# Feed-forward stages of a two-block transformer: modulation rows gathered in one open PSUM bank and turned once per stage

## What is computed

```python
def swiglu(x, w_gate, w_up, w_down):
    return (jax.nn.silu(x @ w_gate) * (x @ w_up)) @ w_down
x = x + 0.5 * swiglu(rms_norm(x, g[0]), ffn_w_gate[layer, 0], ...)
```

```python
sh1, sc1, g1, sh2, sc2, g2 = split_mod(silu(c) @ w_mod[i] + b_mod[i], (B, 1))
ch1, cc1, cg1, ch2, cc2, cg2 = split_mod(silu(c_ctx) @ w_mod[i] + b_mod[i], (1, 1))
```

## Time and profile before

| | |
|---|---|
| median of 3 runs | 4479.57 us |
| lowest and highest run | 4478.26 and 4483.99 us |
| time of the profiled execution | 4477.89 us |
| its span, first to last instruction | 4475.9 us |
| mean granted TensorE clock over the span | 0.962 |
| PE busy | 4127.0 us (92%) |
| PEld busy | 3776.9 us (84%) |
| DVE busy | 3072.6 us (69%) |
| ACT busy | 1807.9 us (40%) |
| moved from and to HBM | 783.44 MB, mean 175 GB/s |

### The profile page before, as it was taken

The page is one execution under the profiler, slowest core; times in us unless marked ns, Lnnn a source line. Parts: engine busy times, 40 slices in busy tenths (PEclk is TensorE's granted clock), DMA queues, the critical chain, the costliest instruction groups (busy, mean ns, idle before and its releaser), DMA issues. The chain is left out here.

```text
span 4475.9 us, 80834 instructions
## 1 busy us (share of the span) xinstructions
PE 4127.0 (92%) x30028; PEld 3776.9 (84%) x30028; DVE 3072.6 (69%) x5251; ACT 1807.9 (40%) x2650; POOL 37.9 (1%) x54
## 2 busy tenths in 40 slices
PE   8978999969988589999999899999997889999998
PEld 8956999949974389899888798998886589899887
DVE  5575565545532637988788588878884659887887
ACT  4324343334331434444333444443333444444333
POOL 0000000000000001000000010000000001000000
PEclk9988999989999989999999999999998999999999
DMA  6633766517530037655777476557772157556775
GB/s 230 211 121 107 229 201 226 184 46 228 170 115 19 4 122 206 194 176 177 227 234 235 157 219 188 177 176 233 235 235 83 43 172 229 170 174 197 235 235 184
DMA packets 299941, 783.44 MB, mean 175 GB/s; under 512 B 32800, under 2 KB 133152, under 8 KB 298912
## 3 DMA queue, kind: packets, MB, share of 16 engines
q1 hardware_dynamic: 299680, 779.81, 56.5%
HBM read 728.29 MB, written 51.38 MB: 174 GB/s over the span
## 5 line engine op out<-in xcount | busy, mean ns | idle before, releaser
L248 ACT ACTIVATE ring_hi<-ring 128x1024 fp32r<-128x1024 f32 x1163 | 1232.7, 1061 | 1926.4 <-PE banks L269 1236.1
L254 DVE TENSOR_TENSOR ring_lo<-ring,ring_hi 128x1024 fp32r<-128x1024 f32 x1163 | 1423.6, 1225 | 658.7 <-ACT ring_hi L248 643.3
L265 PE MATMUL banks<-h_parts,ring_hi 128*128 128x256 f32 x4824 | 1222.5, 291 | 106.2 <-ACT ring_hi L248 104.9
L266 PE MATMUL banks<-h_parts,ring_hi 128*128 128x256 f32 x4824 | 1199.5, 286 | 0.0
L265 PEld LDWEIGHTS banks<-h_parts,ring_hi 128*128 128x128 f32 x4824 | 937.6, 194 | 120.5 <-issue 70.7
L266 PEld LDWEIGHTS banks<-h_parts,ring_hi 128*128 128x128 f32 x4824 | 939.0, 195 | 0.3
L280 PE MATMUL banks<-h_parts,ring_hi 128*128 128x512 f32 x3048 | 763.6, 392 | 0.3 <-DVE h_parts L1681 0.3
L269 PE MATMUL banks<-h_parts,ring_lo 128*128 128x256 f32 x4824 | 681.9, 284 | 0.9 <-DVE ring_lo L254 0.6
L280 PEld LDWEIGHTS banks<-h_parts,ring_hi 128*128 128x128 f32 x3048 | 548.2, 189 | 99.4 <-issue 1.4
L269 PEld LDWEIGHTS banks<-h_parts,ring_lo 128*128 128x128 f32 x4824 | 627.3, 193 | 2.5 <-DVE ring_lo L254 2.5
L283 PEld LDWEIGHTS banks<-h_parts,ring_lo 128*128 128x128 f32 x3048 | 415.8, 190 | 29.7
(11 more groups left out here) (213 smaller groups left out, 3746.6 us busy)
## 6 DMA issues: line engine op xcount, KB each, us to landing
ring<-peer_u_dram SPq DMA_DIRECT2D x384, 512.0 KB, 4.1
ring<-peer_v_dram SPq DMA_DIRECT2D x384, 512.0 KB, 4.2
act_store<-acts_out SPq DMA_DIRECT2D x384, 128.0 KB, 3.2
scratch<-act_store SPq DMA_DIRECT2D x384, 128.0 KB, 3.8
ring<-ffn_gate_dram SPq DMA_DIRECT2D x88, 512.0 KB, 3.9
ring<-ffn_up_dram SPq DMA_DIRECT2D x88, 512.0 KB, 3.7
ring<-ffn_down_dram SPq DMA_DIRECT2D x88, 512.0 KB, 3.7
big<-mod_w_dram SPq DMA_DIRECT2D x80, 512.0 KB, 4.6
```

The source lines that it names most:

```text
L248: self.nc.scalar.activation(self.hi[:, n % 2], self.ring[:, self.slot(j)], ACT.Copy).then_inc(self.count("tile_hi").sem, 1)
L254: self.nc.vector.tensor_tensor(self.lo[:, self.slot(j)], self.ring[:, self.slot(j)], self.hi[:, n % 2].bitcast(F32), ALU.subtract).then_in ...
L265: self.nc.tensor.matmul(out, w, b_hi, start=opens and m == 0, stop=False)
L266: self.nc.tensor.matmul(out, w, b_lo, start=False, stop=False)
```

## The change

`modulate(g)` keeps its eight matmuls, but their weights are a window of 32 columns that begins 8 - 2g columns ahead of chunk c's block of 32, in which the two columns of c now stand at 8 and 9. So c and c_ctx appear in columns 2g and 2g + 1 of the window, and each group adds into two rows of its own, the other rows receive zeros. No matmul has `start` set any more: bank 6 is opened with the other four at the start of the stage, and all five groups add into it. It no longer waits for the copy of the group before.

Copy, turn and bias happen once for a stage, at `kept_at = L + 1` = 21: one copy of bank 6, four turning matmuls whose moving operand `side` has 10 columns in place of 2, and on DVE five bias adds, one for each group, each reading two of every ten columns of bank 7. `vec` and `con` grow by 8 columns each: `after_lam`, zeros behind `lam` into which the last windows reach, and the wider `side`.

```diff
-    ("c", KD * 2), ("ev_sink", 8), ("swa_sink", 16), ("lam", 4 * HD),
+    ("c", KD * 2), ("ev_sink", 8), ("swa_sink", 16), ("lam", 4 * HD), ("after_lam", 8),
...
-for _name, _n in (("ident", P), ("block", P), ("rot", P), ("iota", P), ("cos", T), ("sin", T), ("side", 2)):
+for _name, _n in (("ident", P), ("block", P), ("rot", P), ("iota", P), ("cos", T), ("sin", T), ("side", 10)):
...
-        return self.v("lam").rearrange("p (c m) -> p c m", m=32)
+        return self.v("lam").rearrange("p (c m) -> p c m", m=32)[:, :, 8:10]
+
+    def c_in_row(self, c, g):
+        first = VEC["lam"][0] + 32 * c + 8 - 2 * g
+        return self.vec[:, first:first + 32]
...
-    def group_kept(f):
-        return group_made(f - 1) if f else None
+    kept_at = L + 1
...
             def modulate(g):
-                pe.wait_ge(copied.sem, copied.after(g))
                 pe.wait_ge(landed[g % 2].sem, landed[g % 2].after(16 * RING * (g // 2 + 1)))
                 for c in range(KD):
                     q, r, m = c % 4, c // 2, c % 2
-                    last = nc.tensor.matmul(k.ps[32 * q:32 * q + 32, 6], c_wide[:, c],
-                                            mod_w[g % 2][:, r, m * RING * P:(m + 1) * RING * P], start=c < 4, stop=c >= 4)
+                    last = nc.tensor.matmul(k.ps[32 * q:32 * q + 32, 6], k.c_in_row(c, g),
+                                            mod_w[g % 2][:, r, m * RING * P:(m + 1) * RING * P], start=False,
+                                            stop=g == G - 1 and c >= 4)
                 last.then_inc(modded.sem, 1)
-            def turn(g):
-                pe.wait_ge(copied.sem, copied.after(g + 1))
-                pe.wait_ge(taken.sem, taken.after(g))
+            def turn():
+                pe.wait_ge(copied.sem, copied.after(1))
                 for r in range(RING):
-                    last = nc.tensor.matmul(k.ps[:, 7, 2 * r:2 * r + 2], k.scratch[:, r * P:(r + 1) * P],
+                    last = nc.tensor.matmul(k.ps[:, 7, 2 * G * r:2 * G * (r + 1)], k.scratch[:, r * P:(r + 1) * P],
                                             k.c("side"), start=True, stop=True)
                 last.then_inc(turned.sem, 1)
-            k.open_banks(range(4))
+            k.open_banks((0, 1, 2, 3, 6))
             for f in range(FT):
                 rise(f)
                 if f:
                     fall(f - 1)
-                if group_kept(f) is not None:
-                    turn(group_kept(f))
+                if f == kept_at:
+                    turn()
                 if group_made(f) is not None:
                     modulate(group_made(f))
...
-                g = group_kept(f)
-                if g is not None:
-                    act.wait_ge(modded.sem, modded.after(g + 1))
-                    act.wait_ge(turned.sem, turned.after(g))
+                if f == kept_at:
+                    act.wait_ge(modded.sem, modded.after(G))
                     nc.scalar.activation(k.scratch[:, 0:RING * P], k.ps[:, 6], ACT.Copy).then_inc(copied.sem, 1)
...
-                g = group_kept(f)
-                if g is not None:
-                    at = groups[g] * RING
-                    dve.wait_ge(turned.sem, turned.after(g + 1))
-                    nc.vector.tensor_tensor(mods[:, at:at + RING], k.ps[:, 7, 0:2 * RING].rearrange("p (r m) -> p r m", m=2),
-                                            bias[:, at:at + RING].unsqueeze(2).to_broadcast([P, RING, 2]),
-                                            ALU.add).then_inc(taken.sem, 1)
+                if f == kept_at:
+                    dve.wait_ge(turned.sem, turned.after(1))
+                    rows = k.ps[:, 7, 0:2 * L].rearrange("p (r g m) -> p r g m", g=G, m=2)
+                    for g in range(G):
+                        at = groups[g] * RING
+                        last = nc.vector.tensor_tensor(mods[:, at:at + RING], rows[:, :, g],
+                                                       bias[:, at:at + RING].unsqueeze(2).to_broadcast([P, RING, 2]), ALU.add)
+                    last.then_inc(taken.sem, 1)
```

More of the change, by code:

```diff
@@ L82, in _constants @@
     put("iota", np.broadcast_to(i, (P, P)))
-    put("side", i[:, None] % 32 == np.arange(2))
+    put("side", i[:, None] % 32 == np.arange(10))
     t = np.arange(T)
@@ L714, in swiglu @@
     acc = k.ps[:, 0:4].rearrange("p b (c t) -> p (b c) t", t=T)
-    c_wide = k.c_wide()
     mods, bias = k.mods[:].rearrange("p l n m -> p (l n) m"), k.v("b_mod")
     mod_w = [k.region(8192 + s * RING * D, RING, D) for s in range(2)]
-    assert L < FT - 1
+    assert L < FT - 1 and len(set(groups)) == 5
     def gate_at(f):
@@ L806, in _ @@
             if gain is not None:
-                pe.wait_ge(taken.sem, taken.after(G))
+                pe.wait_ge(taken.sem, taken.after(1))
                 for c in range(KD):
@@ L887, in swiglu @@
         s.ends(FT)
-    for s in (modded, copied, turned, taken):
-        s.ends(G)
+    modded.ends(G)
+    for s in (copied, turned, taken):
+        s.ends(1)
     for m in range(2):
@@ L1808, in _ @@
             dve.wait_ge(copied.sem, copied.after(2))
-            nc.vector.tensor_copy(k.c_wide()[:, :, 0:2], k.v("c").rearrange("p (c m) -> p c m", m=2))
+            nc.vector.tensor_copy(k.c_wide(), k.v("c").rearrange("p (c m) -> p c m", m=2))
         @block.scalar
@@ L2044, in layouts @@
         "c": np.stack([_columns(i["c_2"]), _columns(i["c_ctx_2"])], axis=-1).reshape(P, -1),
-        "ev_sink": rows(_paired(i["ev_sinks"], 8, 4)), "swa_sink": rows(_paired(i["swa_sink_2"], 16, 4)), "lam": rows(i["diff_lambda_2"]),
+        "ev_sink": rows(_paired(i["ev_sinks"], 8, 4)), "swa_sink": rows(_paired(i["swa_sink_2"], 16, 4)), "lam": rows(i["diff_lambda_2"]), "after_lam": np.zeros((P, 8), np.float32),
     }
```

## The result

The changed kernel took 4450.89 us (median of 6 runs, 4443.15 to 4456.26) against 4478.91 us (median of 6, 4476.13 to 4483.99) for the one before: ratio 0.9935, 95% interval 0.9922 to 0.9948. The direction was right, the size was not.

A forecast was written before the change was run, and what follows sets the result against it. PE's instruction queue was taken to bound the four feed-forward stages; -14.5 for turns, +0.9 for opening matmuls and +1.3 for adds gave -12.3 us, from 4479.6 to about 4467 us, range about 4461 to 4475.

The forecast's parts named there:

- the wider constants: Loads of `vec` and `con` 4 KB longer, under 0.1 us, and tiles behind them shifted by 64 bytes: both taken as 0.
- Removed turns: 16 of 20 turns leave PE's queue in the four feed-forward stages, 0.905 us each: -14.5 us.
- opening: One more opening matmul on PE at each of four stage starts, 0.21 us each: +0.9 us.
- adds: Four more bias adds on DVE ahead of the last low part at each stage's end, 0.08 us each: +1.3 us.
- Copies and adds taken off ACT and DVE at no gain: 16 copies on ACT and 16 bias adds on DVE removed inside the stages: nothing gained, since both engines have slack.
- Columns of the turn: The turn at a stage's end has 10 moving columns in place of 2: at most 0.4 us, taken 0.
- Products unchanged: The 20 groups keep 16 passes each on PE, 2.05 us a group: change taken as 0.
- third rival: Products in a group run one after the other, not side by side: +97 us, 4564 us in all; chance 0.03.
- first rival: TensorE's clock falls after the longer pause at all four stage ends: 4.3 us more, gain 8.0, 4471.6 us; chance 0.08.
- second rival: PE waits for `ring_hi` where it now turns: time near 4479.6 us, plus up to 2 us; chance 0.08.

The follow-up runs named there:

- the kernel with only this part: The changed kernel with 192 bytes left free ahead of `hidden_parts`, so that it begins on a multiple of 256 bytes again: 4467.49 us, ratio 0.9975.
- the repetition: The changed kernel measured and profiled once more, unaltered: 4450.42 us, ratio 0.9936 against the kernel before.

## Why the prediction was wrong

- **The step that failed** is this one, on the wider constants: "Tiles behind them in SBUF shift by 64 bytes; nothing in the profile gives that a price", taken as 0. It is worth 10.2 us by the stages and 11.7 and 12.7 by two medians: `hidden_parts` moved from 128 to -64 bytes from the weights, and each of its matmuls began about 5 ns sooner behind the one ahead of it. The change in effect bundles two: the one that it describes, and a move of `hidden_parts`. I saw the second and priced it by the absence of a row. An absent row called for bounds on both sides. That the shift went the same way as the rest is luck; nothing in the working gave it a sign.
- **Removed turns**, 0.905 us each from the pace of the steps, **opening**, 0.21 each, and **adds**, 0.08 each: right. Together they made 3.09 us a stage in the kernel with only this part, against 3.1. The price of an add came out at (0.37 - 0.08) / 4 = 0.07 us: the low part starts 0.37 us behind the first of five adds. By the Trainium skill's 133 ns ("VectorE: DVE Perf Modes", section on the TRN2 errata) with no overlap, an estimate of 5 x 0.133 = 0.67 us; the measurement decides. The prediction took that page's section on the DRAIN as speaking against an overlap. The same section of the Trainium skill adds that a next operation that is not held starts earlier, and the 0.37 us agree with that.
- **Copies and adds taken off ACT and DVE at no gain**: nothing speaks against it; PE shows no wait inside a stage before or after.
- **Columns of the turn**, 10 for 2: 0, right (119 ns a pass in both).
- **Products unchanged**: right, 38.5 us of busy time in both, although none sets `start` any more. The third rival (overlap lost) did not happen.
- **Clock at the stages' ends** (first rival): it fell once before, in the fourth stage, 1.5 us, and twice after, in the first and the third, 1.3 and 1.6 us; in the repetition once, in the third, 1.4 us. The longer pause did not make it fall each time. The rival's price of a fall was right. Its case, all four, did not occur, but part of it did: 1.4 us more than before in the first profile. Too few stages were profiled to say whether the longer pause makes a fall more likely.
- **The time comes back as a wait** (second rival): no. Even at 111 us less, PE's waits of this line for high parts are the ones of before (105 us in 10 waits).
- **The range** held only what I had listed. With the 12 us that the shift turned out to be worth as its bound, it would have reached down to about 4449, and the measured 4450.89 would lie inside.

## What to carry to other kernels

Read a diff for what it does to addresses too: a table made 32 bytes wider moves every tile behind it. When PE is the bound, compare the pitch of one kind of matmul before and after before crediting the edit, and test a gain by making the edit and its layout separately. Where weights and moving operand both stream from SBUF, try their relative starts in steps of 32 or 64 bytes; here that was worth more than any reordering of work.

## What the runs showed of the hardware

- The pitch of full fp32r matmuls of 256 columns (128 x 128 weights, loaded anew for each) depends on how far the moving operand's start lies from the weights'. At 64 bytes below (modulo 256) a plain step of 72 such matmuls, of which 24 read `hidden_parts`, lost 0.125 us, 5 ns on each of the 24 from about 120; for `hidden_parts` -32, -96 and +64 took at most 1.7 us off the 163.4 of its group where -64 took 3.7 to 5.3, while `h_parts` won 1.7% at +64 and 3.6% at -64 against 0. So the sign of 64 has a different weight for the two tiles. Nor does the distance alone say all: at +64 from the low weights the group of `h_parts` took 670.9 us in one layout and 651.7 in another, which was run once. With 512 moving columns -64 was the slowest of the three: 771.4 us, against 763.6 at 0 and 760.0 at +64. Which part of the path gives rise to it is not shown: only places were varied. The Trainium skill, "SBUF — State Buffer", section on operand start alignment, says that an operand may start at any multiple of its element size, and that this is about legality, not speed; by that, the runs here agree and add to it: places that this rule treats alike differ by 1.8% of the kernel's time, 4369.39 against 4447.93 us for the same work.
- Small bias adds of 128 x 8 out of one PSUM bank start about 0.08 us apart (five take 0.46 us), though each is listed as 0.16 long.
- The windowed mixer goes with the granted clock in it: 202.2 us at 0.82 before, 201.7 at 0.83 in the repetition, 196.0 at 0.86 in the changed kernel, 194.3 at 0.88 in the one with 64 bytes ahead of `ring_hi`. The two profiles of the changed kernel differ by 5.7 us there and by 0.6 us in the whole time (4451.17 and 4451.79). So a difference of a few us in such a stage is no evidence.
